# Second block: output product by token tiles between the transposes, last projection in halves, two VectorE steps later

## The chip, the cores and the metric

One Trainium2 chip, one NeuronCore. The metric is the device time of one launch in microseconds; the number given is the median of the runs. All data are float32. TensorE (PE) is the matmul engine, VectorE (DVE), ScalarE (ACT) and GpSimd (POOL) work on rows, SyncE (SP) issues the loads of weights.

## The reference

Two blocks of two layers each on x of 256 tokens by 1024. The first block (pooling and windowed attention, then 128 retrieved experts of 16384 per token) isn't touched. The second block is, per layer:

```
proj = rms_norm(x) @ w_in[l]                      # 2400 columns
y_a = mla_mixer(...)    # 4 heads; q and k of 96, latent ranks 192 and 128
y_b = diff_mixer(...)   # 4 heads, two maps each, w = p0 - lam * p1, rms per head
y_c = swa_mixer(...)    # 4 heads, window of 128, sinks
y_d = na_mixer(...)     # 4 heads, neighbourhood with relative bias
mix = concat(norm(y_a), y_b, norm(y_c), norm(y_d))   # 4 sections of 256
x = x + mix @ w_out[l]
x = x + square(relu(rms_norm(x) @ w_up[l])) @ w_down[l]   # width 4096
```

After two layers a last rms_norm gives the output.

## The kernel before

Each engine has its own program, written out in order by hand (`pe_program` from L561, `act_program` from L1040, `dve_program` from L1412, `sp_program`), and they meet at semaphores: `up` counts one, `at` names the count to wait for. An engine never passes an instruction that waits. Tokens lie in two tiles of 128, t=0 and t=1. L565 is the helper `mm` for all matmuls; each of its calls shows as two matmul instructions in the trace. L677 is the transposes of attention maps (`p_transposes`), L907 those of the mixed output (`mixed_T`), L644 those of the normed input (`transposes`). On VectorE L1420 is the copy helper, L1424 the tensor-tensor helper, L1429, L1430 and L1434 scale. On ScalarE L1044 is the copy helper, L1120 the exponential.

In the second block the attention has ten groups in the order d0 d1 d2 d3 (differential), m0 m1 (latent), w0 w1 (window), n0 n1 (neighbourhood). They run in twelve rounds r (loops over `range(12)` in all three programs). TensorE in round r issues the scores of group r, the products with the values of group r-3, then a projection or other piece that belongs to the round, then the transposes of the maps of group r-2. A d group has one PSUM bank of transposes, copied by ScalarE alone. The others have two, bank 0 copied by ScalarE and bank 1 by VectorE (`evac_pT`), and the values of the group wait for both. Scores of group r wait until the scores bank of group r-2 has been read: by the exponentials on ScalarE for d and m, by the bias on VectorE for w and n.

VectorE in round r: bias and maximum of group r-1, sums of group r-2 (for d groups they end the map), a piece of the round, the values of group r-3 into Y (`attended`), more pieces, then its bank of transposes of group r-2. ScalarE in round r: exponentials of group r-1, a piece of the round (in round 9: the copy of projection D2), then its bank of transposes of group r-2.

The projection comes in blocks of 256 columns, B0 B1 B2 C0 C1 D0 D1 D2. C1 (round 2) holds keys and values of the window groups, D2 (round 9) the values of the neighbourhood groups. D2 is 32 matmul instructions: 8 chunks of the contraction, for each half of the tokens, two instructions each. Its evacuation waits for both halves (`pe.prj`).

The output product (`out2`) adds four sections in PSUM: section s, tile t goes to banks 2t and 2t+1, 8 instructions of 512 columns. Each section is transposed first (`mixed_T`), and copied into HT by ScalarE (a, c) or VectorE (b, d). Sections c and d wait for their norms: squares on ScalarE, scaling on VectorE. When section d of a tile is done, VectorE adds the banks to x, ScalarE takes the squares, VectorE scales into H (`v.n2`), TensorE transposes it, and ScalarE and VectorE copy half of it each to HT. Then the widening (`widen`) of the feed-forward begins: for its first two blocks, 0 and 1, by tiles, later for both tiles at once. Each block is followed by relu on ScalarE; the widening of block 2 waits for the relu of block 1.

Single PSUM banks come from a ring of four (`singles`), handed out in the order of the calls; a taker waits until the last holder's data was read. Weights come through a ring of twelve 1 MB slots (`in_2`), loaded by SP in the order of the program; each load waits for the last use of its slot (for `w_out` that of tile 1, `pe.out2, l, s, 1`). The feed-forward multiplies pairs of 256-wide blocks with seven products in place of eight, with sums of weights and of activations made on VectorE.

Of the kernel before, what the change touches and what calls it, by code (L numbers as in the profile page):

```python
# [11 lines left out]
ALU = mybir.AluOpType  # L12
# [61 lines left out]
class Tally:  # L74
# [23 lines left out]
    def at(self, name, *idx):  # L98
        sem = self.named(name)
        return sem, 1 if self.dry else self.value[(name, *idx)]  # L100
# [88 lines left out]
def build(nc, I, out):  # L189
    with ExitStack() as ctx:  # L190
# [370 lines left out]
        def pe_program(e):  # L561
# [108 lines left out]
            def p_transposes(g, P):  # L670
                pe.wait_ge(*at(*(("v.lam", *g.key) if g.lam is not None else ("a.exp", *g.key))))
                for z in range(g.banks):
                    bk, freed = singles.take(("pT", *g.key, z), (engine_of(z) + ".pT", *g.key, z))
                    if freed:
                        pe.wait_ge(*at(*freed))
                    for x, (i, kc) in enumerate(g.pieces(z * 4)):
                        p = pe.e.transpose(PS[:, bk, x * 128:(x + 1) * 128], P[:, i, kc * 128:(kc + 1) * 128], ident)  # L677
                    p.then_inc(*up("pe.pT", *g.key, z))
# [15 lines left out]
            def p_views(ring, g):  # L694
                s = weights(ring, g.key)
                P = s[:, 0:1024].rearrange("p (i k) -> p i k", i=4)[:, 0:g.n, 0:g.keys]
                return (P[:, 0:g.n:2, :] if g.lam is not None else P), s[:, 1024:2048]
# [151 lines left out]
            def project(l, name, parts=(0, 1)):  # L849
                for t in parts if name in FIRST[l] else range(2):  # L850
                    have_hT(2 + l, t, 0)
                w = have(in_2, ("w2", l, name)).rearrange("p (k n) -> p k n", k=8)
                if name in FIRST[l]:
                    bk = singles.where[("prj", l, name)] = FIRST[l][name]
                    if l > 0:
                        pe.wait_ge(*at("v.xf", l - 1, 0))
                else:
                    bk, freed = singles.take(("prj", l, name), (EVAC[name] + ".prj", l, name))
                    if freed:
                        pe.wait_ge(*at(*freed))  # L860
                for z in parts:
                    zs = slice(z * 128, (z + 1) * 128)
                    for k in range(8):
                        if name in ("D0", "D1"):
                            p = mm(PS[:, bk, z * 256:(z + 1) * 256], w[:, k, zs], HT[:, k, :], k == 0, k == 7)
                        else:
                            p = mm(PS[:, bk, z * 256:(z + 1) * 256], HT[:, k, zs], w[:, k, :], k == 0, k == 7)
                if 1 in parts:
                    p.then_inc(*up("pe.prj", l, name))
# [94 lines left out]
            for l in range(L):  # L964
                if l > 0:
                    project_A(l, 0)
                project(l, "B0", (0,))
                project(l, "B1", (0,))
                transposes(2 + l, 1, 0, ("v.n1", l, 1))
                project_A(l, 1)  # L970
                project(l, "B0", (1,))
                project(l, "B1", (1,))
                latent_T(l, 0)
                latent_T(l, 1)
                project(l, "B2")
                slabs_T("dT", l, 0, 4)
                slabs_T("dT", l, 1, 4)
                groups = second_groups(l)
                for r in range(12):
                    if r < 10:  # L980
                        g = groups[r]
                        if g.before:
                            pe.wait_ge(*at(*(("v.bias", *g.before.key) if g.before.biased else ("a.exp", *g.before.key))))
                        else:
                            pe.wait_ge(*(at("v.xe", 1, 1) if l == 0 else at("v.xf", l - 1, 1)))
                            pe.wait_ge(*at("a.prj", l, "B0"))
                            pe.wait_ge(*at("v.prj", l, "B1"))
                        scores(g)
                    if r > 2:
                        values(groups[r - 3], p_views(in_2, groups[r - 3])[1])  # L990
                    if r == 0:
                        lift(l, 0)
                        lift(l, 1)
                    elif r == 1:
                        project(l, "C0")
                    elif r == 2:
                        for t in range(2):
                            pe.wait_ge(*at("a.ukv", l, t))
                            pe.wait_ge(*at("v.mheads", l))
                            heads_T("mT", "av", [QF[:, t, i, :] for i in range(4)] + [KF[:, t, i, :] for i in range(4)], 96, l, t)  # L1000
                        project(l, "C1")
                    elif r == 4:
                        slabs_T("wT", l, 0, 3)
                        slabs_T("wT", l, 1, 3)
                        project(l, "D0")
                    elif r == 6:
                        project(l, "D1")
                    elif r == 9:
                        project(l, "D2")
                    elif r == 10:  # L1010
                        mixed_T(l, "b")
                        mixed_T(l, "a")
                    if r > 1:
                        p_transposes(groups[r - 2], p_views(in_2, groups[r - 2])[0])
                    if r > 9:
                        for t in range(2):
                            out2(l, "b" if r == 10 else "a", t)
                values(groups[9], p_views(in_2, groups[9])[1])
                mixed_T(l, "c")
                for t in range(2):  # L1020
                    out2(l, "c", t)
                mixed_T(l, "d")
                for t in range(2):
                    out2(l, "d", t)
                for t in range(2):
                    transposes(2 + l, t, 2, ("v.n2", l, t))
                    widen(l, 0, (t,))
                    widen(l, 1, (t,))
                for q in range(8):
                    for part in range(2):  # L1030
                        if q < 7:
                            widen(l, 2 * q + 2 + part, (0, 1))
                        down(l, q, part)
                singles.n = 3
                singles.held = {4: ("v.xf", l, 0), 5: ("v.xf", l, 1), 6: ("v.xf", l, 1), 7: ("a.relu", l, 15)}
                if l == 0:
                    transposes(3, 0, 0, ("v.n1", 1, 0))
# [374 lines left out]
        def dve_program(e):  # L1412
# [499 lines left out]
            for l in range(L):  # L1912
# [30 lines left out]
                for r in range(12):  # L1943
# [24 lines left out]
                    elif r == 2:  # L1968
                        for t in range(2):
                            evac_heads("mT", MT, 1, 4, 4, 96, l, t)  # L1970
                        projected(l, "C1")
                    elif r == 3:
                        for t in range(2):
                            v.wait_ge(*at("pe.dT", l, t))
                        v.wait_ge(*at("a.prj", l, "C0"))
                        wc, ws = turns(64, 32)
                        tmp = RT[:, 0:768].rearrange("p (t n) -> p t n", t=2)
                        rope(five(RB[:, :, 0:384], 6), five(prj2[:, :, X_SQ:X_SQ + 384], 6), 6, wc, ws, five(tmp, 6))
                        tt(RB[:, :, 0:384], RB[:, :, 0:384], tmp, ALU.add).then_inc(*up("v.wrope", l))
                    elif r == 4:  # L1980
                        slabs("wT", WT, l, 1, 3)
                    elif r == 6:
                        projected(l, "D1")
                    if r > 2:
                        if r < 5:
                            v.wait_ge(*at("pe.hT", 2 + l, groups[r - 3].t, 0, 1))
                        attended(groups[r - 3])
                    if r == 7:
                        yb = Y[:, :, 256:512].rearrange("p t (i d) -> p t i d", i=4)
                        jb = RT[:, 0:512].rearrange("p (t i d) -> p t i d", t=2, i=4)  # L1990
                        tt(jb, yb, yb, ALU.mult).then_inc(*up("v.c"))
                        own()
                        v.e.reduce_sum(sc("yb", 8), RT[:, 0:512].rearrange("p (i d) -> p i d", i=8), AX).then_inc(*up("v.subs", l))
                    if r == 9:
                        scaled(l, "a")
                        q = inverse("yb", 8, ("yb", l)).rearrange("p (t i) -> p t i", t=2)
# [3 lines left out]
                        ins.then_inc(*up("v.yn2", l, "b"))  # L2000
                    if r > 1:
                        evac_pT(groups[r - 2], in_2)
                scaled(l, "c")
                attended(groups[9])
                scaled(l, "d")
# [199 lines left out]
```

## Time and profile before

| | us |
|---|---|
| runs | 2305.83, 2308.43, 2312.58 |
| median | 2308.43 |
| profiled execution, its time | 2297.69 |
| its span | 2295.9 |
| PE busy | 2058.7 (90%) |
| DVE busy | 1338.5 (58%) |
| ACT busy | 828.6 (36%) |
| mean granted clock of PE | 0.976 |

The span is cut in 40 slices by the page; the first 27 belong mostly to the first block, whose last expert product ends near 1564 us. From there on layer 0 of the second block runs to about 1930 us and layer 1 to the end. The table's busy time of PE is modelled: a run of matmuls ends when the last result is out, some 0.2 us behind the time at which the next could have been issued. Idle time of an engine that another one doesn't wait for costs nothing.

### The profile page before, as it was taken

The page shows a single profiled execution, that of the slowest core. Times are in us where ns is not written, and L with a number is a line of the kernel's source. Part 1 is how long each engine was busy: PE and PEld are TensorE (multiplying, and loading weights), DVE is VectorE, ACT ScalarE, POOL GpSimd, SP SyncE. Part 2 cuts the span into 40 slices and gives each one's busy share as a digit, 9 for nine tenths or more (in the row PEclk, how much of TensorE's full clock was granted, in tenths as well). Part 3 has the DMA queues.
Part 4 walks back from the last instruction along what each step waited for, and adds up shares of the span by engine and source line. Part 5 has one row for each costly group of instructions (what it writes and reads, how often), then busy time and mean ns, then how long its engine had stood idle before and what let it go on. Part 6 is the DMA issues. An engine that isn't in the chain of part 4 may idle for free.

```text
span 2295.9 us, 24261 instructions
## 1 busy us (share of the span) xinstructions
PE 2058.7 (90%) x8172; PEld 1226.1 (53%) x8172; DVE 1338.5 (58%) x3057; ACT 828.6 (36%) x2389; POOL 609.2 (27%) x564
## 2 busy tenths in 40 slices
PE   6898998897979888999887888889999999999998
PEld 5564554453535434655443243436757666766665
DVE  2237867988557677786778566754524332544323
ACT  2224644545354344464444444542420001331000
POOL 1124445344444343433443444330000000000000
PEclk9898999998999999999999999999999999999999
DMA  9899999999999999999999999994342342242430
GB/s 372 362 419 427 418 426 426 427 426 422 426 427 422 426 427 424 427 385 427 426 427 421 426 427 427 426 427 182 128 184 110 156 182 71 105 189 93 185 152 19
DMA packets 106017, 750.82 MB, mean 327 GB/s; under 512 B 12034, under 2 KB 12322, under 8 KB 16035
## 3 DMA queue, kind: packets, MB, share of 16 engines
q0 software_dynamic: 80640, 587.24, 60.9%
q1 hardware_dynamic: 25252, 162.03, 17.8%
q8 instruction: 65, 1.06, 0.2%
q14 instruction: 60, 0.49, 0.1%
HBM read 748.17 MB, written 1.05 MB: 326 GB/s over the span
## 4 chain that ended last, share of the span: by engine, by line
PE 54%; DMA 22%; DVE 15%; ACT 6%; issue 2%; POOL 1%; DVEq 0%; ACTq 0%; POOLq 0%
PE PS L565 52%; DMA BIG<-in_uv,EID 18%; DVE BIG L1770 6%; DMA MOD<-in_uv,EID 2%; ACT DG L1044 1%; DMA BIG<-in_wada 1%; ACT L1257 1%; DVE BIG L1424 1%; ACT L1248 1%; DVE BIG L1434 1%; DVE SC L1516 1%; PE PS L677 1%; ACT AV L1044 1%; DVE BIG L1420 1%; PE PS L644 1%
## 5 line engine op out<-in xcount | busy, mean ns | idle before, releaser
L565 PE MATMUL PS<-BIG,DG 128*128 128x512 f32 (+1 forms) x2156 | 898.5, 587 | 152.4 <-ACT DG L1044 129.7
L1770 DVE CUSTOM_DVE_ANT_0 BIG<-BIG,H 128x1024 f32<-128x1024 f32 x455 | 558.2, 1227 | 305.5 <-DMA BIG<-in_uv,EID 276.7
L505 POOL DMA_INDIRECT BIG<-in_uv,EID x455 | 521.9, 1147 | 721.0 <-PE PS L565 691.8
L565 PEld LDWEIGHTS PS<-BIG,DG 128*128 128x128 f32 (+1 forms) x2156 | 341.0, 182 | 607.9 <-issue 305.4
L565 PE MATMUL PS<-HT,BIG 128*128 128x128 f32 (+1 forms) x2304 | 383.9, 323 | 10.4 <-DMA BIG<-in_wq 5.3
L565 PEld LDWEIGHTS PS<-HT,BIG 128*128 128x128 f32 x2304 | 349.5, 193 | 75.2 <-issue 45.1
L1257 ACT ACTIVATE AV<-AV 128x1 f32<-128x1 f32 x512 | 103.1, 201 | 609.4 <-DVE AV L1770 602.4
L565 PE MATMUL PS<-BIG,HT 128*128 128x256 f32 (+3 forms) x1216 | 292.4, 397 | 7.3 <-DVE HT L1424 3.6
L565 PEld LDWEIGHTS PS<-BIG,HT 128*128 128x128 f32 x1216 | 224.6, 191 | 73.0 <-issue 46.2
L1424 DVE TENSOR_TENSOR BIG<-BIG 128x256 f32<-128x256 f32 (+2 forms) x176 | 96.1, 546 | 221.7 <-ACT BIG L1396 216.5
L1044 ACT ACTIVATE DG<-CST,AV 128x128 f32<-128x128 f32 x512 | 205.5, 401 | 48.5 <-ACT AV L1044 1.1
L565 PE MATMUL PS<-BIG 128*128 128x512 f32 (+6 forms) x504 | 164.9, 499 | 1.7 <-DVE BIG L1420 1.7
L1044 ACT ACTIVATE AV<-AV,GATE 128x1 f32<-128x1 f32 x512 | 150.7, 294 | 18.8 <-ACT AV L1257 0.4
L1396 ACT ACTIVATE BIG<-PS 128x512 f32<-128x512 f32 x32 | 19.1, 597 | 350.5 <-PE PS L565 350.5
L565 PE MATMUL PS<-MOD,DG 128*128 128x512 f32 (+1 forms) x276 | 113.9, 569 | 16.8 <-ACT DG L1044 16.7
L565 PEld LDWEIGHTS PS<-BIG 128*128 128x128 f32 (+3 forms) x504 | 79.5, 190 | 66.6 <-issue 62.8
L1770 DVE CUSTOM_DVE_ANT_0 BIG<-MOD,H 128x1024 f32<-128x1024 f32 x57 | 70.1, 1229 | 36.5 <-DMA MOD<-in_uv,EID 32.9
L1044 ACT ACTIVATE BIG<-PS 128x256 f32<-128x256 f32 (+6 forms) x122 | 53.1, 448 | 87.0 <-PE PS L677 46.7
L565 PEld LDWEIGHTS PS<-MOD,DG 128*128 128x128 f32 (+1 forms) x276 | 43.1, 181 | 77.0 <-issue 39.6
L565 PE MATMUL PS<-MOD,BIG 128*128 128x64 f32 (+1 forms) x320 | 81.8, 401 | 1.8 <-DVE BIG L1420 1.7
L505 POOL DMA_INDIRECT MOD<-in_uv,EID x57 | 61.6, 1081 | 75.0 <-PE PS L565 69.6
L565 PEld LDWEIGHTS PS<-MOD,BIG 128*128 128x128 f32 x320 | 47.6, 191 | 37.1 <-issue 36.0
(191 smaller groups left out, 1418.1 us busy)
## 6 DMA issues: line engine op xcount, KB each, us to landing
BIG<-in_wada POOLq DMA_DIRECT2D x43, 1024.0 KB
BIG<-in_wup SPq DMA_DIRECT2D x32, 1024.0 KB, 8.9
BIG<-in_wdn SPq DMA_DIRECT2D x32, 1024.0 KB, 4.9
BIG<-in_win SPq DMA_DIRECT2D x31, 1024.0 KB, 5.0
BIG<-in_wout SPq DMA_DIRECT2D x24, 1024.0 KB, 5.5
BIG<-in_wq SPq DMA_DIRECT2D x23, 1024.0 KB
BIG<-in_uv,EID POOLq DMA_INDIRECT x455
MOD<-in_wada POOLq DMA_DIRECT2D x5, 1024.0 KB
```

The lines of the kernel that those rows point to most:

```text
L505: pool.e.indirect_dma_start(out=slot(u), out_offset=None, in_=I[f"uv{l}"], in_offset=bass.IndirectOffsetOnAxis(ap=EID[:, t * 128 + j:t * 1 ...
L565: return pe.e.matmul(dst, a, b, start=start, stop=stop)
L644: p = pe.e.transpose(PS[:, bk, c * 128:(c + 1) * 128], H[:, t, (c4 * 4 + c) * 128:(c4 * 4 + c + 1) * 128], ident)
L677: p = pe.e.transpose(PS[:, bk, x * 128:(x + 1) * 128], P[:, i, kc * 128:(kc + 1) * 128], ident)
L1044: return a.e.activation(dst, src, ACT.Copy, scale=scale)
L1248: a.e.activation(GATE[:, j:j + 16], V[:, 32:48], ACT.Exp, bias=V[:, 48:49], scale=1.0, accum_out=V[:, 49:50]).then_inc(*up("a.gate", l, t, h))
L1257: a.e.activation(AV[:, j:j + 1], AV[:, j:j + 1], ACT.Gelu).then_inc(*up("a.gelu", p, b - 1))
L1420: return v.e.tensor_copy(dst, src)
L1424: return v.e.tensor_tensor(dst, a, b, op)
L1434: return v.e.scalar_tensor_tensor(out=dst, in0=a, scalar=s, in1=b, op0=op0, op1=op1)
L1516: v.e.reduce_max(mx, src, AX).then_inc(*up("v.c"))
L1770: v.e.tensor_tensor_reduce(out=JD, in0=slot(u)[:, 0:1024], in1=H[:, t, :], scale=1.0, scalar=0.0, op0=ALU.mult, op1=ALU.add, accum_out=AV[ ...
```

## The change

TensorE: `project` can be called with one half after the other, and takes its bank with the first. D2's first half stands before the transposes of round 9, its second half behind them. The output product is issued by tiles: b of tile 0 behind the transposes of round 10, b of tile 1 behind those of round 11, then values of group 9, transposes of c, a of tile 0, transposes of d, c and d of tile 0, a and c of tile 1, transposes of the normed tile 0, d of tile 1, widening 0 of tile 0, transposes of the normed tile 1, and the other three quarters of the first two widenings. VectorE: the copy of C1 goes from round 2 to round 3, behind the maximum of group 2 and the sums of group 1; the squares of section b go behind the copy of transposes in round 7. ScalarE's and SP's programs are as before.

```diff
@@ project (pe_program)
-                else:
+                elif 0 in parts:
                     bk, freed = singles.take(("prj", l, name), (EVAC[name] + ".prj", l, name))
                     if freed:
                         pe.wait_ge(*at(*freed))
+                bk = singles.where[("prj", l, name)]
                 for z in parts:
@@ rounds (pe_program)
                     elif r == 9:
-                        project(l, "D2")
+                        project(l, "D2", (0,))
                     elif r == 10:
                         mixed_T(l, "b")
                         mixed_T(l, "a")
                     if r > 1:
                         p_transposes(groups[r - 2], p_views(in_2, groups[r - 2])[0])
+                    if r == 9:
+                        project(l, "D2", (1,))
                     if r > 9:
-                        for t in range(2):
-                            out2(l, "b" if r == 10 else "a", t)
+                        out2(l, "b", r - 10)
+
                 values(groups[9], p_views(in_2, groups[9])[1])
                 mixed_T(l, "c")
-                for t in range(2):
-                    out2(l, "c", t)
+                out2(l, "a", 0)
                 mixed_T(l, "d")
-                for t in range(2):
-                    out2(l, "d", t)
-                for t in range(2):
-                    transposes(2 + l, t, 2, ("v.n2", l, t))
-                    widen(l, 0, (t,))
-                    widen(l, 1, (t,))
+                out2(l, "c", 0)
+                out2(l, "d", 0)
+                out2(l, "a", 1)
+                out2(l, "c", 1)
+                transposes(2 + l, 0, 2, ("v.n2", l, 0))
+                out2(l, "d", 1)
+                widen(l, 0, (0,))
+                transposes(2 + l, 1, 2, ("v.n2", l, 1))
+                widen(l, 1, (0,))
+                widen(l, 0, (1,))
+                widen(l, 1, (1,))
@@ rounds (dve_program)
                     elif r == 2:
                         for t in range(2):
                             evac_heads("mT", MT, 1, 4, 4, 96, l, t)
-                        projected(l, "C1")
                     elif r == 3:
                         for t in range(2):
                             v.wait_ge(*at("pe.dT", l, t))
+                        projected(l, "C1")
                         v.wait_ge(*at("a.prj", l, "C0"))
...
                         attended(groups[r - 3])
-                    if r == 7:
-                        yb = Y[:, :, 256:512].rearrange("p t (i d) -> p t i d", i=4)
-                        jb = RT[:, 0:512].rearrange("p (t i d) -> p t i d", t=2, i=4)
-                        tt(jb, yb, yb, ALU.mult).then_inc(*up("v.c"))
-                        own()
-                        v.e.reduce_sum(sc("yb", 8), RT[:, 0:512].rearrange("p (i d) -> p i d", i=8), AX).then_inc(*up("v.subs", l))
...
                     if r > 1:
                         evac_pT(groups[r - 2], in_2)
+                    if r == 7:
+                        yb = Y[:, :, 256:512].rearrange("p t (i d) -> p t i d", i=4)
+                        jb = RT[:, 0:512].rearrange("p (t i d) -> p t i d", t=2, i=4)
+                        tt(jb, yb, yb, ALU.mult).then_inc(*up("v.c"))
+                        own()
+                        v.e.reduce_sum(sc("yb", 8), RT[:, 0:512].rearrange("p (i d) -> p i d", i=8), AX).then_inc(*up("v.subs", l))
```

## Rows read from the trace of the kernel before

**Rows 1.** TensorE's waits, 1600 to 1735 us: total, times, longest.
```profile
PE PS L565 <- DVE BIG L1420: 3.1, 3, 2.1
...
PE PS L644 <- DVE H L1429: 0.4, 1, 0.4
```

**Rows 2.** Windows: length, busy (count) per engine, granted PEclk, DMA share, GB/s.
```profile
1656.00:1660.00 4.00, 4.00 (x21) 3.13 (x20) 3.46 (x9) 2.60 (x11) 0.00 (x0) 0.57 0.00 0
2022.00:2026.00 4.00, 4.00 (x23) 3.35 (x22) 3.05 (x9) 2.59 (x11) 0.00 (x0) 0.64 0.00 0
1740.00:1930.00 190.00, 189.12 (x675) 125.75 (x674) 60.85 (x82) 11.68 (x23) 0.00 (x0) 1.00 0.36 140
```

**Rows 3.** Timeline, round 3: start, length, engine, what, idle before.
```profile
1618.98 0.69 DVE L1420 COPY MOD<-PS 128x512 f32<-128x512 f32 x1 [6.58 <-PE PS L565]
...
1619.42 0.60 ACT L1044 ACTIVATE BIG<-PS 128x512 f32<-128x512 f32 x1 [7.28 <-PE PS L677]
...
1619.59 1.22 DVE L1516 TENSOR_REDUCE SC<-PS 128x4 f32<-128x1024 f32 x1
...
1620.38 1.10 PE L565 MATMUL PS<-MOD,BIG 128*128 128x64 f32 x8
...
1621.04 0.47 ACT L1120 ACTIVATE BIG<-PS,SC 128x256 f32<-128x256 f32 x1 [1.03 <-DVE SC L1429]
...
1622.95 0.66 PE L677 MATMUL PS<-CST,BIG 128*128 128x128 f32 x4 [1.47 <-DVE BIG L1434]
```

**Rows 4.** Timeline, rounds 7 to 9: group 5's maps, group 6's values.
```profile
1652.17 0.69 DVE L1424 TENSOR_TENSOR MOD<-H 128x512 f32<-128x512 f32 x1
...
1653.50 0.57 ACT L1044 ACTIVATE BIG<-PS 128x512 f32<-128x512 f32 x1
...
1654.49 1.22 DVE L1434 SCALAR_TENSOR_TENSOR BIG<-PS,CST 128x1024 f32<-128x1024 f32 x1
...
1654.52 2.09 PE L565 MATMUL PS<-PRJ,BIG 128*128 128x64 f32 x16 [2.09 <-DVE BIG L1420]
...
1660.10 1.86 PEld L565 LDWEIGHTS PS<-MOD,BIG 128*128 128x128 f32 x16 [0.48 <-ACT BIG L1044]
```

**Rows 5.** Timeline, rounds 9 and 10: D2 and what follows it.
```profile
1661.94 7.13 PE L565 MATMUL PS<-BIG,HT 128*128 128x256 f32 x32
...
1669.10 0.60 ACT L1044 ACTIVATE MOD<-PS 128x512 f32<-128x512 f32 x1 [3.07 <-PE PS L565]
...
1670.81 1.97 PE L565 MATMUL PS<-MOD,BIG 128*128 128x64 f32 x16 [0.87 <-DVE BIG L1420]
...
1673.58 0.69 DVE L1420 COPY HT<-PS 128x512 f32<-128x512 f32 x1
...
1674.87 0.66 PE L677 MATMUL PS<-CST,BIG 128*128 128x128 f32 x4 [0.78 <-DVE H L1424]
```

**Rows 6.** Timeline, output product and widening.
```profile
1675.36 7.03 PE L565 MATMUL PS<-BIG,HT 128*128 128x512 f32 x16
...
1682.23 1.89 PE L565 MATMUL PS<-MOD,BIG 128*128 128x64 f32 x16
...
1695.07 7.10 PE L565 MATMUL PS<-BIG,HT 128*128 128x512 f32 x16 [1.02 <-ACT HT L1044]
...
1703.48 7.11 PE L565 MATMUL PS<-BIG,HT 128*128 128x512 f32 x16 [0.87 <-DVE HT L1424]
...
1707.19 1.29 DVE L1424 TENSOR_TENSOR X<-PS,X 128x512 f32<-128x512 f32 x2 [3.85 <-PE PS L565]
...
1711.03 1.09 PE L644 MATMUL PS<-CST,H 128*128 128x128 f32 x8 [0.44 <-DVE H L1429]
...
1712.96 7.22 PEld L565 LDWEIGHTS PS<-HT,BIG 128*128 128x128 f32 x64 [1.08 <-issue]
...
1722.12 7.38 PE L565 MATMUL PS<-HT,BIG 128*128 128x128 f32 x64 [0.87 <-ACT HT L1044]
...
1730.28 4.99 PE L565 MATMUL PS<-HT,BIG 128*128 128x256 f32 x22 [0.78 <-ACT BIG L1396]
```

## Prediction

> **What bounds the kernel now.** I read the busy tenths and PE's groups of the page first, then PE's waits in the second block, then the order of time around each. The time before 1560 us (weights, experts' rows from memory) is untouched. From there to the end TensorE is the path: in the feed-forward of layer 0, PE is busy 189.12 of 190 us, with the DMA engines at a 0.36 share [rows 2]. So only PE's waits in the two attention stages can be won. In layer 0 its waits from 1600 to 1735 us are seven rows that sum to 10.3 us, the largest 3.1 and the smallest 0.4 [rows 1]; layer 1 shows the same places 366 us later, each within 0.1 us (seen on its own timeline). I work out layer 0 and double it. Groups 0 to 9 are d0 d1 d2 d3 m0 m1 w0 w1 n0 n1; round r scores group r, transposes r-2 and takes the values of r-3.
>
> **C1 later on VectorE (round 3).** Before, VectorE stands at the copy of C1 until TensorE has finished C1 at 1618.94; the maximum of group 2, whose scores were ready near 1609.8, starts only at 1619.59, then the sums of group 1, and TensorE waits for these from 1621.5 to 1622.95 [rows 3]. After, the maximum (1.22) and the sums of group 1 (from 1620.92 to 1622.9, 2.0) run before C1 is done. TensorE issues the 8 value products from 1620.38 in 0.94, so the transposes start at 1621.32; 4 of them take 0.44. What is late next is the scores of group 4, which wait for the four exponentials of group 2 on ScalarE. They start at 1621.04 now, because of the maximum [rows 3]; then they start at 1619.92, half a microsecond behind the start of the copy before them, and take 4 x 0.47 = 1.9: ready at 1621.85, seen by PE near 1621.95. The scores started at 1623.45 in the trace, so the gain is 1.5; with 0.1 that the two slab transposes lose now, I take **1.55**. Bounds: 0 if ScalarE's order undoes it, 1.7 if nothing is late next. The copy of C1 itself stays at 1618.98, so who waits for its bank loses nothing. The rope behind it ends near 1622.6 and is used at 1624.4.
>
> **The squares of section b later (round 7).** TensorE waits until 1654.52 for group 5's transposed maps. VectorE's half could be copied at 1652.17, where the squares stand, 1.5 earlier. But ScalarE's half is copied at 1653.50 for 0.57, behind the exponentials of group 6: ready at 1654.07, so PE restarts at 1654.22, 0.3 earlier. And that is lost at once: VectorE's total is the same, the bias of group 7 still starts at 1654.49, ScalarE follows it, and PE's next values start at 1660.10 at ScalarE's release [rows 4]. I take **0**, bounds 0 and 0.3.
>
> **D2 in halves (round 9).** D2's 32 instructions take 6.96 from 1661.94; 8 transposes follow (0.88), then the values wait until 1670.81: 1.0 lost. The second half, 3.45, is now behind the transposes and could hide this wait. It doesn't, because ScalarE's order is unchanged: it waits for all of D2, copies it, and only then copies its half of the transposed maps, in that order already in the trace at 1669.10 (two copies 0.5 apart, 0.60 long) [rows 5]. D2 now ends 0.88 later, at 1669.95. Copies start at 1669.98 and 1670.48, end at 1671.08, PE restarts at 1671.22: 0.41 later than before. VectorE's half is long done, and the maximum of group 9 runs some 3 us earlier, so the copy of section b (1673.58 before, when VectorE came free, while its transposes, issued from 1672.61, were done at 1673.2) starts when the transposes are done, 1673.67. The wait for the freed bank at 1674.87 then ends at 1674.96. Of the 0.41 there is left **+0.09**. Bounds: +0.41 (nothing absorbed) and -1.0 (were ScalarE not behind D2).
>
> **The output product and the widening.** Waits on this piece are 1.02 and 0.87 (each behind one section's transposes), 0.44, 0.87, 0.87 [rows 6], 4.07 idle. A wait also costs the drain of the last result, which a queue without wait overlaps: beside the 0.87 the weight loads show 1.08. Start to start they cost 1.19, 1.04, 0.68, 1.08, 1.03, together 5.0. One t-half of a section is half of 6.87 (1675.36 to 1682.23), 3.43; group values 1.73; 8 transposes 0.88; a quarter of the widening 3.61 (7.22/2). From 1675.45 the new order is: b0 to 1678.88, values 8 to 1680.61, transposes 9 to 1681.49, b1 to 1684.93, values 9 to 1686.66, c transposed to 1687.10, a0 to 1690.53. Section d has to be scaled: squares on ScalarE behind its copy of c, then VectorE, in the trace 3.45 us from c's transposes to d scaled, so ready at 1690.1: no wait, by 0.4. d transposed to 1690.97, c0 to 1694.41, d0 to 1697.84, a1 to 1701.28, c1 to 1704.71. The addition, norm and scaling of tile 0 take 3.86 from d0's end (1707.17 to 1711.03), done by 1702: hidden. Transposes to 1705.59, d1 to 1709.03 (drained 1709.27); the HT copies hide under it. Widening quarter to 1712.64. Tile 1 is ready 3.86 after 1709.27, at 1713.13: **0.5 is late there**, the one wait left. Then transposes and three quarters to 1724.84; the relu wait stays (1730.28 against 1729.33, 0.95), so the next block starts at 1725.79 instead of 1730.28: **-4.5**, the +0.09 of D2 included. Each t-half has its own banks, tile 0's HT columns are read by no product after d0, so nothing new waits for those. ScalarE's mixed c and d stand in the same order. Bounds -3.6 (d's scaling and tile 1 each 0.4 later) and -5.1. On SP the load that reuses a's slot comes later, a1 ending 9.6 us after the a of now (1691.7); its weights are for a block after 1755, so it is hidden.
>
> **Sum.** Per layer -1.55 - 4.5 = -6.05, two layers **-12.1 us**. The profiled execution would go from 2297.69 (span 2295.9) to 2285.6. The median shown, 2308.43, lies 10.7 above that execution; nothing in the change touches what differs between them, so 2308.43 - 12.1 = **2296.3**.
>
> **TensorE's clock.** The granted clock is 0.57 in 1656 to 1660, behind the 2.09 wait, and 0.64 in 2022 to 2026: about 3.4 us at the lower level (1.2 GHz) in layer 0. PE there has slack until ScalarE's release at 1660.10, so it costs nothing now [rows 2, 4]. The 0.3 shorter wait leaves PE idle about as much. The Trainium skill, "TensorE: Matmul & The Clock Gate", Part 1, says that the observation that lowers the clock runs free of the kernel's own start; by that the low stretch could fall a little later, on D2. By the trace the cost is 0.
>
> **Rivals.**
> 1. The low stretch lands on D2 or the output product, which have no slack: 3.4 us at half speed lose 1.7 per layer, 3.4 in both: 2299.7, gain 8.7. For it: D2 follows directly, and PE at full clock would now idle 1.9 us more before 1660.10. Against: neither layer of the trace shows it. The page's free-running observation gives the same time.
> 2. Only the output part works: ScalarE's exponentials hold round 3 at its old pace (0 for C1), and the tail gives 3.6: 7.2 in both: 2301.2. For it: ScalarE's chain is within 0.1 us of PE's in round 3. Against: its release (the maximum) is plainly earlier.
> 3. The full hiding of D2 and of the squares' wait: 1.0 + 1.5 more per layer: 17.1, 2291.3. Against: both need ScalarE to be earlier than its rows allow.
> 4. Slower: the feed-forward waits for its weights. Loads are issued in order on SP, and the slot of a is freed 9.6 - 1.55 = 8 us later than now. It decides if those weights land after their block begins (some 55 us of margin), or if the feed-forward is paced by loads; then each layer ends up to 8 us later: +16.1, 2324.5. Against: the DMA share of 0.36 and one PE wait of 0.9 in 190 us.
>
> **Chances.** Forecast 0.62, rival 1 0.19, rival 2 0.10, rival 3 0.05, rival 4 0.04. The forecast's own range is 2292 to 2301: terms 1.2 to 1.7 and 3.9 to 5.1 per layer give 10.2 to 13.6, and three runs spread 6.8 us, so some 3 on each side. All together 2289 to 2304. A measurement of this kernel tells about 0.3%, 7 us, from no change. Faster holds the forecast and rival 3, most of 1 and half of 2: 0.83; same 0.13; slower 0.04.
>
> **What would show it.** Right: no wait before the transposes of group 1 in round 3; values of group 5 about 0.3 earlier while values of group 6 still begin at ScalarE's release; a ScalarE copy of D2 that begins only behind the second half, and a wait of 1.2 to 1.4 before the values of group 7; no wait behind the transposes of c and d, and one of 0.3 to 0.5 before tile 1's transposes; the feed-forward 6 us earlier in layer 0 and 12 in layer 1. Wrong: a wait for weights in the feed-forward; lower clock beside D2; section d scaled later than a0's end.

## The result, and the profile after

| | before | after |
|---|---|---|
| median of the runs, us | 2308.01 (4 runs, 2305.83 to 2312.58) | 2290.64 (4 runs, 2288.25 to 2292.18) |
| ratio, 95% interval | | 0.9927 [0.9899, 0.9955] |
| again, five rounds: median, us | 2304.90 (24 runs) | 2289.49 (6 runs) |
| ratio, 95% interval | | 0.9937 [0.9922, 0.9952] |
| profiled execution: time, span, us | 2297.69, 2295.9 | 2292.18, 2290.4 |

Faster: by the medians 17.4 us in the first comparison and 15.4 in the second (by the ratios 16.8 and 14.5). 12.1 was forecast. The two profiled executions lie only 5.5 apart. To see why, I cut each span at four marks of TensorE: the second of the two input products of layer 0 (64 instructions of 192 columns), the first full widening, and the same two in layer 1. The time from the first mark of a layer to its second is called its attention here.

| us | to mark 1 | attention 0 | feed-forward 0 | attention 1 | feed-forward 1 |
|---|---|---|---|---|---|
| before | 1572.9 | 157.37 | 208.64 | 157.39 | 199.6 |
| after | 1575.6 | 152.11 | 208.64 | 154.43 | 199.6 |
| after, second trace (`e_after` below) | 1571.6 | 154.43 | 208.63 | 151.12 | 199.6 |
| forecast for after | as before | 151.3 | as before | 151.3 | as before |

The feed-forward is the same to 0.01 us, so the time before it, 2.7 more in this execution and 1.3 less in the next, is scatter of the first block. The attention is where the change is, and its time isn't one number: 151.1 at best (6.25 under before; two layers 12.5), and up to 3.3 more. A layer whose attention is at its best is called undisturbed below. The rest of the section takes the stage in order.

Round 3, timeline (start, length, engine, what, idle before), answering to [rows 3]. This execution is 2.69 us behind the other at the value products of round 3:

```profile
1615.01 1.21 DVE L1523 TENSOR_REDUCE SC<-PS 128x4 f32<-128x1024 f32 x1
...
1621.67 0.69 DVE L1427 COPY MOD<-PS 128x512 f32<-128x512 f32 x1 [3.35 <-PE PS L565]
...
1622.60 0.47 ACT L1127 ACTIVATE BIG<-PS,SC 128x256 f32<-128x256 f32 x1
...
1623.07 1.10 PE L565 MATMUL PS<-MOD,BIG 128*128 128x64 f32 x8
...
1624.01 0.60 PE L677 MATMUL PS<-CST,BIG 128*128 128x128 f32 x4
...
1624.58 1.99 PE L565 MATMUL PS<-BIG 96*128 96x256 f32 x8
...
1627.91 7.07 PE L565 MATMUL PS<-HT,BIG 128*128 128x256 f32 x32
```

D0 in the trace of before:

```profile
1626.79 7.07 PE L565 MATMUL PS<-HT,BIG 128*128 128x256 f32 x32
```

VectorE takes the maximum of group 2 at 1615.01, far ahead of the copy of C1 (1621.67, still where TensorE ends it). The exponentials start at 1622.60, right behind the start of ScalarE's copy, and the transposes of group 1 have no wait. From the value products to the start of D0 it was 6.41 (1620.38 to 1626.79) and is 4.84 (1623.07 to 1627.91).

Rounds 7 to 9, answering to [rows 4]:

```profile
1653.35 0.69 DVE L1427 COPY BIG<-PS 128x512 f32<-128x512 f32 x1
...
1654.08 0.69 DVE L1431 TENSOR_TENSOR MOD<-H 128x512 f32<-128x512 f32 x1
...
1654.62 0.57 ACT L1051 ACTIVATE BIG<-PS 128x512 f32<-128x512 f32 x1
...
1655.24 2.20 PE L565 MATMUL PS<-PRJ,BIG 128*128 128x64 f32 x16 [1.69 <-ACT BIG L1051]
...
1661.22 2.00 PE L565 MATMUL PS<-MOD,BIG 128*128 128x64 f32 x16 [0.42 <-ACT BIG L1051]
```

The copy of the maps on VectorE stands ahead of the squares, and now ScalarE's (1654.62) is the releaser: 1.69 of wait in place of 2.09. The values of group 6 begin 5.98 behind those of group 5, where before it was 5.58: what was gained, 0.40, is given back.

D2 and the round behind it, answering to [rows 5]:

```profile
1663.06 3.67 PE L565 MATMUL PS<-BIG,HT 128*128 128x256 f32 x16
...
1666.57 1.04 PE L677 MATMUL PS<-CST,BIG 128*128 128x128 f32 x8
...
1667.44 3.62 PE L565 MATMUL PS<-BIG,HT 128*128 128x256 f32 x16
...
1671.10 0.60 ACT L1051 ACTIVATE MOD<-PS 128x512 f32<-128x512 f32 x1 [3.94 <-PE PS L565]
...
1671.59 0.59 ACT L1051 ACTIVATE BIG<-PS 128x512 f32<-128x512 f32 x1
...
1672.28 2.12 PE L565 MATMUL PS<-MOD,BIG 128*128 128x64 f32 x16 [1.22 <-issue]
...
1674.19 1.91 PE L908 MATMUL PS<-CST,H 128*128 128x128 f32 x8
```

ScalarE copies D2 at 1671.10, and its half of the transposed maps, finished on TensorE at 1667.6, only at 1671.59. The values wait 1.22 ("issue" here: the profile names no releaser at that place; the copy ends 0.10 before them, at 1672.18). Then the 8 transposes at 1674.19 last 1.91 where the 8 at 1666.57 last 1.04.

Output product and widening, answering to [rows 6]:

```profile
1691.55 0.62 DVE L1436 TENSOR_SCALAR H<-H,SC 128x256 f32<-128x256 f32 x2
...
1692.59 0.60 PE L908 MATMUL PS<-CST,H 128*128 128x128 f32 x4
...
1693.03 13.90 PE L565 MATMUL PS<-BIG,HT 128*128 128x512 f32 x32
...
1706.76 1.04 PE L644 MATMUL PS<-CST,H 128*128 128x128 f32 x8
...
1711.27 1.29 DVE L1431 TENSOR_TENSOR X<-PS,X 128x512 f32<-128x512 f32 x2 [2.75 <-PE PS L565]
...
1715.11 1.09 PE L644 MATMUL PS<-CST,H 128*128 128x128 f32 x8 [0.30 <-DVE H L1436]
...
1716.04 10.88 PE L565 MATMUL PS<-HT,BIG 128*128 128x128 f32 x96
...
1727.70 7.14 PE L565 MATMUL PS<-HT,BIG 128*128 128x256 f32 x32 [0.78 <-ACT BIG L1403]
```

Section d is scaled at 1692.17, 0.4 ahead of its transposes; c, d of tile 0 and a, c of tile 1 are one run of 32 from 1693.03; tile 1's transposes wait 0.30; three quarters of the widening follow without a wait. From round 11's transposes to the first full widening it is 45.04 (1682.66 to 1727.70); before it was 46.32 (1683.96 to 1730.28), though half a section, 3.43, more is left to do at that point now: 4.7 less.

The rest is told by windows with a granted clock under 0.99 (columns as in [rows 2]); the first of them answers to the one at 1656 there:

```profile
1656.00:1660.00 4.00, 4.00 (x24) 3.59 (x24) 3.56 (x9) 1.48 (x6) 0.00 (x0) 0.61 0.00 0
...
1672.00:1676.00 4.00, 3.72 (x25) 3.75 (x26) 0.71 (x2) 0.18 (x1) 0.00 (x0) 0.74 0.98 344
...
1676.00:1680.00 4.00, 4.00 (x15) 2.62 (x14) 1.36 (x4) 3.40 (x11) 0.00 (x0) 0.83 1.01 426
...
2020.00:2024.00 4.00, 2.04 (x10) 2.04 (x11) 3.70 (x5) 3.98 (x13) 0.00 (x0) 0.76 0.02 4
...
2024.00:2028.00 4.00, 4.00 (x15) 3.46 (x15) 2.61 (x11) 3.85 (x12) 0.00 (x0) 0.50 0.00 0
...
2028.00:2032.00 4.00, 4.00 (x22) 3.51 (x21) 0.72 (x3) 0.00 (x0) 0.00 (x0) 0.88 0.00 0
```

The wait ahead of the stretch in layer 1:

```profile
2021.96 3.57 PE L565 MATMUL PS<-MOD,BIG 128*128 128x64 f32 x16 [2.02 <-ACT BIG L1051]
```

A share x of a window at the lower level (1.2 GHz) shows as 1 - x/2. An unbroken time at that level is called a low stretch below. So 0.61 at 1656 is 3.1 us, part of a stretch on work that is followed by slack, as in the kernel before. 0.74 and 0.83 are 3.4 us, on the values, transposes and first output product of round 10 in layer 0; 0.76, 0.50 and 0.88 are 6.9 us, on the values of group 6 and the first half of D2 in layer 1. There TensorE is the path, and the two cost 1.0 and 3.3 over 151.1.

### The profile page after: what moved, and what is told of

It is laid out like the page before. It is cut to its first block, busy times and chain, and to the rows that moved or that the text cites. A ratio compares the mean times of both kernels' runs of the same rounds, so it can differ in the third digit from the quotient of the medians.

```text
span 2290.4 us, 24261 instructions
## 1 busy us (share of the span) xinstructions
PE 2059.0 (90%) x8172; PEld 1225.7 (54%) x8172; DVE 1338.8 (58%) x3057; ACT 827.7 (36%) x2389; POOL 610.1 (27%) x564
## 4 chain that ended last, share of the span: by engine, by line
PE 55%; DMA 22%; DVE 14%; ACT 6%; issue 2%; POOL 0%; DVEq 0%; ACTq 0%; POOLq 0%
PE PS L565 54%; DMA BIG<-in_uv,EID 19%; DVE BIG L1777 6%; DMA MOD<-in_uv,EID 2%; ACT DG L1051 1%; DMA BIG<-in_wada 1%; ACT L1264 1%; DVE BIG L1431 1%; ACT L1255 1%; PE PS L677 1%; ACT AV L1051 1%; ACT BIG L1127 1%; PE PS L644 1%; DVE BIG L1441 1%; DVE BIG L1427 0%
## 5 line engine op out<-in xcount | busy, mean ns | idle before, releaser
L565 PE MATMUL PS<-MOD,DG 128*128 128x512 f32 (+1 forms) x276 | 118.9, 597 | 16.9 <-ACT DG L1051 16.8
```

Source lines behind the costliest of these rows:

```text
L565: return pe.e.matmul(dst, a, b, start=start, stop=stop)
```

## The experiments

**The change again, and its parts.** The first four ran on the same chip in the same rounds. First the changed kernel itself.

> The changed kernel again, beside the kernel before in the same rounds. My sum: 12.1 us less (ratio 0.9948), the low-clock stretches adding up to 1.7 each. If the -17 of the first comparison is the change itself, the ratio is near 0.9925. The trace of the second block should keep every wait of the first one (1.7 before the values of group 5, 1.22 before those of group 7, 0.3 before tile 1's transposes); if the clock's low stretches are not tied to the work, they fall elsewhere than in the first trace.

Measured: 2289.49, ratio 0.9937 [0.9922, 0.9952]; six runs within 4.6. Each wait is there again (1.69, 1.22, 0.31). The low stretches fell elsewhere: on group 6's values and D2 in layer 0, behind a wait of 2.03 (154.43), and on work with slack in layer 1 (151.12). So 151.12 is the undisturbed layer; the forecast had 151.3.

Only the order of output product and widening:

```diff
-                        for t in range(2):
-                            out2(l, "b" if r == 10 else "a", t)
+                        out2(l, "b", r - 10)
...
+                out2(l, "a", 0)
                 mixed_T(l, "d")
...
```

> Only the order of the output product and of the first two widenings; D2 whole, both VectorE pieces where they were. By my steps: 4.6 us per layer, 9.2 in all, ratio 0.9960. Rival (the tail gives only what is left of the waits, 3.6 per layer): 7.2, ratio 0.9969. The other three edits then account for the difference to the whole change.

Measured: 2294.54, ratio 0.9963 [0.9949, 0.9977]. Attention 152.66 and 152.66: 4.7 less per layer, 9.4 in both. My step said 4.6 for this kernel; the rival with 3.6 is out.

Only C1:

```diff
                     elif r == 2:
...
-                        projected(l, "C1")
                     elif r == 3:
...
+                        projected(l, "C1")
```

> Only C1's copy moved to round 3. By my step: 1.55 us per layer, 3.1 in all, ratio 0.9987; the transposes of group 1 follow the value products without a wait. Rival (ScalarE's order holds the old pace): 0, ratio 1.0000, and a wait before the scores of group 4 of about 1.5.

Measured: 2297.90, ratio 0.9968 [0.9952, 0.9984]. Attention 155.81 and 155.80: 1.57 per layer, against 1.55 forecast, and no wait before the scores of group 4. But the median is 7 us lower, and by the interval the gain is at least 3.7, so 3.1 lies outside. The edit does more than take a wait away; see below. Alone, C1 gives 1.57 and the output part 4.71 per layer, together 6.28; the whole change gives 6.25. So D2 in halves and the later squares are worth nothing together, to 0.03.

Only D2 in halves:

```diff
-                        project(l, "D2")
+                        project(l, "D2", (0,))
...
+                    if r == 9:
+                        project(l, "D2", (1,))
```

> Only D2 in halves. By my step: nothing gained, 0.1 us per layer lost (0.41 at the values of group 7, 0.3 of it absorbed), ratio 1.0001; ScalarE's copy of D2 stands before its copy of the maps and the wait is 1.2 to 1.3 in place of 0.87. Rival (the second half hides the wait): 1.0 per layer gained, ratio 0.9991, no wait before the values of group 7.

Measured: 2307.67, ratio 1.0003 [0.9982, 1.0025]: nothing gained. The wait is 1.22 in both layers and from group 6's values to group 7's it takes 11.06 in place of 10.71. The 0.3 that VectorE's earlier maximum should give back can't be seen in this trace, because in both layers a low stretch (granted 0.57 and 0.62 over 4 us) stands on round 10; attention took 158.42 and 159.98, the second with a further stretch behind round 3. In the changed kernel's undisturbed layer it is seen: the wait for the freed bank is 0.45 in place of 0.78.

**ScalarE's order.** The changed kernel, with this:

```diff
@@ rounds (act_program)
-                    elif r == 9:
-                        projected(l, "D2")
                     if r > 1 and r != 10:
                         evac_pT(groups[r - 2], in_2)
+                    if r == 9:
+                        projected(l, "D2")
```

> The changed kernel, and ScalarE copies its half of group 7's maps before D2. Theory: ScalarE's order alone keeps the second half of D2 from hiding the wait. Then no wait before the values of group 7, the undisturbed layer is 1.4 us shorter than the 151.1 of the changed kernel (149.7), and no low-clock stretch falls in round 10 any more; 2.8 us and up to 1.7 per stretch in all, ratio to before 0.992 to 0.993. Rival (PE waits there for VectorE or for a bank): the wait stays at 1.2, ratio as the changed kernel's 0.9937.

Measured: 2287.01, ratio 0.9911 [0.9884, 0.9938], on another chip than the last. The interval just holds the rival's 0.9937, so the trace has to decide. Its timeline:

```profile
1668.90 0.60 ACT L1051 ACTIVATE BIG<-PS 128x512 f32<-128x512 f32 x1 [3.44 <-PE PS L677]
...
1669.07 3.62 PE L565 MATMUL PS<-BIG,HT 128*128 128x256 f32 x16
...
1672.53 1.89 PE L565 MATMUL PS<-MOD,BIG 128*128 128x64 f32 x16
...
1672.73 0.60 ACT L1051 ACTIVATE MOD<-PS 128x512 f32<-128x512 f32 x1 [3.24 <-PE PS L565]
```

The maps are copied at 1668.90, under D2's second half, and the values follow it at once: 3.46 from the start of that half to the values, where the changed kernel takes 4.84. So 1.4 per layer were to be had here, and it was ScalarE's order alone that kept them. Both layers took 152.99, though, not 149.7: the wait before group 6's values, 2.03, stayed, and a low stretch on them and on D2 cost the 3.3 between the two in each (16 value instructions last 3.13 and 2.96 there, 2.00 at the full clock). None fell in round 10.

**The squares earlier.** The changed kernel, but VectorE takes the values of group 3 and the squares in round 6, ahead of its wait of 7.9 us for D1:

```diff
@@ rounds (dve_program)
-                    elif r == 6:
-                        projected(l, "D1")
                     if r > 2:
...
                         attended(groups[r - 3])
+                    if r == 6:
+                        yb = Y[:, :, 256:512].rearrange("p t (i d) -> p t i d", i=4)
...
+                        projected(l, "D1")
...
-                    if r == 7:
-                        yb = Y[:, :, 256:512].rearrange("p t (i d) -> p t i d", i=4)
...
```

> The changed kernel, but VectorE takes the values of group 3 and the squares of section b before it waits for D1 (round 6) instead of behind the transposes of round 7. Theory: rounds 7 to 9 are bound by VectorE's total from D1's copy on, so 1.9 us leave the path: the values of group 6 start 1.9 earlier against D1, the wait before them falls from 2.0 to about 0.7, the undisturbed layer takes 149.2 in place of 151.1. 3.8 us in all and fewer low-clock stretches, ratio 0.991 to 0.992. Rival (it is ScalarE's exponentials that bind, whatever VectorE does): 0.4 per layer at most, ratio 0.9935.

Measured: 2285.84, ratio 0.9910 [0.9883, 0.9936]; attention 150.22 and 151.57, the second with a low stretch in round 10. The wait before group 6's values is gone altogether. Layer 0 is 0.9 shorter, more than the 0.4 at most of the rival, which fits VectorE's total as the bound of these rounds; by its interval the median alone wouldn't tell them apart. But 0.9 came, not 1.9; the next run's rows show where the rest went.

**Both.**

> Both of these edits on the changed kernel. Theory: they act at different waits and add: undisturbed layer 151.1 - 1.4 - 1.9 = 147.8, in all 6.6 us under the changed kernel, more if the low stretches go with the waits: ratio to before 0.990 to 0.991. Rival (once one wait is gone the other hides less): no better than the better of the two, 0.992.

Measured: 2280.40, ratio 0.9893 [0.9864, 0.9921], the fastest of all and 5.4 under the better of the two, beside which it ran; attention 148.80 and 149.11 in place of 147.8. Rounds 7 to 9 of it:

```profile
1645.03 0.69 DVE L1427 COPY BIG<-PS 128x512 f32<-128x512 f32 x1 [5.16 <-PE PS L565]
...
1651.26 1.23 DVE L1441 SCALAR_TENSOR_TENSOR BIG<-PS,CST 128x1024 f32<-128x1024 f32 x1
...
1652.35 2.18 PE L565 MATMUL PS<-PRJ,BIG 128*128 128x64 f32 x16 [1.53 <-ACT BIG L1051]
...
1654.32 1.91 PE L677 MATMUL PS<-CST,BIG 128*128 128x128 f32 x8
...
1656.25 0.57 ACT L1051 ACTIVATE BIG<-PS 128x512 f32<-128x512 f32 x1
...
1657.84 2.00 PE L565 MATMUL PS<-MOD,BIG 128*128 128x64 f32 x16
```

ScalarE releases group 6's maps at 1656.82, nearly as it should (1.8 earlier against D1's copy), but the values start at 1657.84. The transposes at 1654.32 last 1.91 and the scores behind them are slow too: the low stretch still stands behind a wait (1.53), and with no slack left after it, it is paid for. D1's copy in the trace of before:

```profile
1646.49 0.69 DVE L1420 COPY BIG<-PS 128x512 f32<-128x512 f32 x1 [7.87 <-PE PS L565]
```

From there to group 6's values (1660.10) it took 13.61, and here it takes 12.81 (1645.03 to 1657.84): 0.8 of the 1.9. That the missing part is the stretch is argued from these rows; no layer of this kernel was seen without one.

**The clock, and the long runs.** The kernel before, under its own name:

> The kernel before under a name of its own: a second trace of it. Ratio 1.0000 within about 0.15%. From TensorE's second input product to the first full widening each layer should take 157.4 us again if the low-clock stretch stays where PE has slack (theory: in this kernel the 2.1 wait before the values of group 5 draws the stretch onto work that is followed by slack); if its place is chance, a layer that has it on D2 takes up to 1.7 more.

Measured: 2306.84, ratio 1.0014 [0.9993, 1.0035]; attention 158.86 and 157.39: in layer 0 the stretch reached D2. Five of its twelve runs took over 2310 us, with mean granted clocks of 0.966 to 0.970; its fastest, 2297.93, had 0.975. Three single executions followed: two of the kernel before, one of the changed one.

> One look at the kernel before, for the place of its low-clock stretches. Theory: a stretch of 3.4 us at the lower level falls behind one of TensorE's waits (1.5 in round 3, 2.1 in round 8, 0.9 in round 9, the five of the output part) and costs up to 1.7 where PE has no slack; the layers take 157.4 plus 0 to 3.5. Rival: the runs above 2310 us lose their time in the first block, and the layers take 157.4 whatever the run's time.

> A second look, same expectations: layers of 157.4 plus up to 3.5 (clock behind waits), or 157.4 in every run (rival).

> A further look at the changed kernel. Theory: layers of 151.1 undisturbed, up to 3.4 more where a low stretch begins in the wait before the values of group 6 and runs into D2, or behind the 1.2 wait before those of group 7; no low stretch behind round 10, where no wait over 0.8 is left. Rival: low stretches fall in the output part too.

The first of them caught a long one: 2307.89, with attention of 162.22 and 162.14, the feed-forward as ever 208.63 and the first block 1573.5. The second was 2299.27 with 158.89 and 157.40. The changed kernel took 2288.97 with 152.11 and 154.38. The long execution's windows in layer 0, behind the 2.09 wait:

```profile
1656.00:1660.00 4.00, 4.00 (x20) 3.60 (x21) 3.29 (x9) 1.98 (x8) 0.00 (x0) 0.53 0.00 0
...
1660.00:1664.00 4.00, 4.00 (x20) 3.26 (x17) 3.18 (x6) 3.95 (x12) 0.00 (x0) 0.50 0.00 0
...
1664.00:1668.00 4.00, 4.00 (x14) 3.37 (x14) 2.68 (x8) 2.65 (x9) 0.00 (x0) 0.50 0.00 0
...
1668.00:1672.00 4.00, 4.00 (x16) 3.38 (x15) 0.00 (x1) 0.00 (x0) 0.00 (x0) 0.76 0.02 4
```

and in layer 1, behind the 1.5 wait of round 3:

```profile
1992.00:1996.00 4.00, 2.53 (x14) 2.30 (x15) 3.75 (x11) 2.37 (x9) 0.00 (x0) 0.77 0.00 0
...
1996.00:2000.00 4.00, 4.00 (x14) 3.34 (x13) 3.76 (x8) 0.98 (x4) 0.00 (x0) 0.50 0.01 2
...
2000.00:2004.00 4.00, 4.00 (x15) 3.55 (x15) 3.02 (x7) 1.61 (x7) 0.00 (x0) 0.50 0.63 203
...
2004.00:2008.00 4.00, 4.00 (x19) 3.47 (x19) 1.93 (x6) 0.00 (x0) 0.00 (x0) 0.95 0.45 190
```

That is 13.7 us at the lower level in layer 0 and 10.2 in layer 1, costing 4.8 in each. So in this long run the excess sits in the attention, and round 3's wait is one of the places where a stretch begins. Of 70 timed runs of the kernel before (under either name) in the three comparisons with five rounds, 18 took over 2310 us; of 12 with D2's halves alone, 3; the 7 with the output part alone spread over 11 us. Of 12 with C1's edit alone none was over 2302.8, and the 11 of the changed kernel lie between 2287.19 and 2292.18. It isn't the whole story: the kernel with both further edits has C1's edit too, and one of its six runs took 2289.51, 7.6 over the next. The last kernel puts C1 back into the changed one:

```diff
                     elif r == 2:
...
+                        projected(l, "C1")
                     elif r == 3:
...
-                        projected(l, "C1")
```

> The changed kernel with C1's copy put back in round 2. Theory: the 1.5 wait in round 3 does two things: it costs 1.57 a layer, and it is a place where a long low-clock stretch can begin. So an undisturbed layer takes 152.7, and the runs spread upward again: the slowest some 8 to 15 us over the fastest, where the changed kernel's eleven runs lay within 5; the median 5 to 8 us over the changed kernel's 2289.5, ratio to before 0.995 to 0.998. Rival (the long stretches are drawn by the output part's waits, which stay away here): median 3.1 over, 2292.6, spread 5, ratio 0.9945 to 0.995.

Measured: 2293.64, ratio 0.9957 [0.9937, 0.9976]; 12 runs from 2289.93 to 2303.96. The layer without a costly stretch took 152.72, as expected. The spread is back (14 in place of 5); the median is 4.2 up on the changed kernel's, between the two theories' numbers, and from another comparison; the ratio is within the theory's range, but the interval holds the rival's too. The trace caught a stretch right behind the wait of round 3:

```profile
1624.00:1628.00 4.00, 3.75 (x12) 3.10 (x13) 3.76 (x8) 0.86 (x3) 0.00 (x0) 0.59 0.01 4
```

Its layer took 155.28, with a further costly stretch in round 10 (1675.9 to 1679.3). If that one cost 1.0, as in the changed kernel, some 1.6 is left for the stretch of round 3.

**Where a stretch falls.** Read in windows of 1 us, all 14 traces have a low stretch in each of their two layers that begins 0 to 2.3 us after TensorE resumes from the wait before group 5's values or the one before group 6's. In the changed kernel this decides the time. Where it fell behind group 5's values (layer 0 of the first trace), the next wait was 0.42 instead of 2.02 and this stretch cost nothing; where it fell on group 6's values, it was 6.9 us long and cost 3.3. A stretch began behind round 3's wait in 3 of the 14 layers that have this wait, and in none of the 14 without it.

## Why the prediction was right

- Size and sign: 12.1 forecast, 12.5 from undisturbed layer to undisturbed layer. The measured 17.4 and 15.4 are more, and 2290.64 lies just under the forecast's own range of 2292 to 2301. It is next to rival 3's 2291.3, by chance: what rival 3 asks for, no wait before the values of group 7, isn't in the traces (1.22). In these runs, the kernel before has long ones that the changed one hasn't; its median in the second comparison lies 7 above its fastest run, the changed kernel's 2.3 above its own. My sum started from one profiled execution that happened to have no costly stretch, and I took its distance to the median, 10.7, as nothing to do with the change. That was the wrong sentence: of a long run's distance, 9.6 was low stretches in the attention, and C1's edit removes a place where they begin. That this makes up the 3 to 5 us between 12.5 and the medians is argued from that one long trace and the spread of the runs, not shown.
- C1: 1.55 forecast, 1.57 measured with this edit alone, and ScalarE's exponentials late next, by 0.2 at the weight loads, as said.
- Squares of b: 0 forecast. PE restarts 0.40 earlier, not 0.3, and it is all lost at group 6's values. Right, and the run with the squares under D1 fits the reason: the order in which VectorE does its share doesn't matter there, the amount does. The edit was never run alone; that it is worth nothing rests on the sum of the parts.
- D2: a loss of 0.41 before absorption; 0.35 measured (1.22 of wait). The 0.3 given back by the earlier maximum is there (0.78 to 0.45). With ScalarE's two copies exchanged 1.4 per layer come out.
- Output part: 4.5 forecast, 0.09 of D2's loss within it; 4.7 measured with this part alone, against my 4.6. Of its single statements, the margin of 0.4 for section d was 0.4, and the wait before tile 1, 0.5 start to start, was 0.43 (1711.07 + 3.61 to 1715.11; 0.30 idle in the view).
- Rival 1 (clock) happened. I gave it 0.19 beside the forecast as if it were another outcome; it is a term of the sum, in both kernels: over their undisturbed layers the changed kernel's three traces carry 4.3, 3.3 and 4.3 us of it, four of the kernel before 0, 1.5, 9.6 and 1.5. Its price was right in kind and up to twice as large (3.3 in a layer, 6.9 us long). The statement that it can hit D2, since PE is idle 1.9 us more before group 6's values, held; that wait is 2.02 where the clock is full.
- Rivals 2, 3 and 4 didn't occur; no wait for weights in either feed-forward.

Open: why a stretch lasts 3.4 us in one execution and 13.7 in another, and how often each kernel has the long kind; that would need many more traces. That C1's wait draws it is not shown: it rests on three layers that have one behind it (layer 1 of the long run and of the kernel with only D2 halved, layer 0 of the last kernel) and on the spread of the runs.

## What to carry to other kernels

When a wait is filled by moving work of the waiting engine, look at the order of the engine that must release it: a copy that now ends later may stand in front of the one that is wanted. Work taken off a chain's engine while that engine is idle (the squares under D1) shortens the chain; exchanging two pieces within a chain that is bound by its total doesn't (0.40 gained and lost again in round 7), while exchanging ScalarE's two copies did, since only the order held back the one that was wanted. And price a TensorE wait like the ones here (1.2 to 2.1 us) as wait plus what the clock may take from the work behind it, which is hidden only where slack follows.

## What the runs showed of the hardware that was not expected

The granted clock fell to the lower level behind single waits of 1.2 to 2.1 us, with TensorE at work before and after them. It did not in the feed-forward of layer 0 with its one wait of 0.9 in 190 us (some traces have a stretch in the last 10 us of the run, where it costs nothing: feed-forward 1 takes 199.6 in all), and in no trace behind the waits of 0.9 to 1.0 in the output part. It did not always fall during the wait: in layer 1 of the changed kernel it was full from 2020 to 2022, with TensorE idle, and 0.56 from 2022 to 2023, with TensorE at work again; in layer 0 it fell at 1674.0, 1.7 us after the values had started. The Trainium skill, "TensorE: Matmul & The Clock Gate", Part 1, has the clock return to half rate after TensorE has been idle; the traces agree in that each stretch looked at in this text stands behind a wait. The stretches measured were 3.4, 6.9, 10.2 and 13.7 us long. The same part of the Trainium skill also says that the observation runs free of the kernel; the traces agree in that the same instructions were hit in one execution and spared in the next.
